# A streaming-encoder trunk in float32 on one core: four kinds of DVE blocks put behind the wide weight splits of their chunk

## The reference

```
h      = rmsnorm(x);  proj = h @ w_in
o_a    = sparse attention with an indexer (8 heads of 128)
o_b    = sliding-window attention (16 heads of 64, sinks)
gates  = sigmoid(h @ w_gate)                  # 2 x 2048 columns: g_a, g_b
merged = g_a * (o_a @ w_branch_a) + g_b * (o_b @ w_branch_b)
x      = x + merged @ w_out
x      = x + square(relu(rmsnorm(x) @ w_up)) @ w_down     # 2048 -> 8192 -> 2048
```

## Time and profile before

| what | us |
|---|---|
| median of three runs | 2659.25 |
| the profiled execution | 2660.85 |
| span of its trace (first to last instruction) | 2659.0 |
| PE busy | 2646.0 |
| PEld busy | 2219.8 |
| DVE busy | 2080.4 |
| ACT busy | 1451.0 |

### The profile page before, as it was taken

One profiled execution on the slowest core, in us unless ns is written; L12 is line 12 of the kernel. 1 busy time (PEld: TensorE's weight loads), 2 busy tenths in 40 slices (PEclk: granted clock), 3 DMA queues, 4 the chain that ended last, 5 costly groups with the idle time before them and its releaser, 6 DMA issues.

```text
span 2659.0 us, 37301 instructions
## 1 busy us (share of the span) xinstructions
PE 2646.0 (100%) x13432; PEld 2219.8 (83%) x13432; DVE 2080.4 (78%) x3099; ACT 1451.0 (55%) x1863; POOL 233.0 (9%) x408
## 2 busy tenths in 40 slices
PE   9999999999999999999999999999999999999998
PEld 7788778888888888888888887788888888888887
DVE  5677678977898997987756766789678989989875
ACT  5545555545565655645455455555456556556554
POOL 0103110000100100100010021100000001000000
PEclk9999999999999999999999999999999999999999
DMA  7887775776775766767677677667677767667574
GB/s 248 240 240 223 224 227 188 226 237 235 237 230 190 246 219 207 241 205 237 227 238 226 223 226 224 215 199 235 221 247 240 224 204 245 211 215 229 195 248 152
DMA packets 185092, 594.52 MB, mean 224 GB/s; under 512 B 25576, under 2 KB 43540, under 8 KB 184784
## 3 DMA queue, kind: packets, MB, share of 16 engines
q1 hardware_dynamic: 161936, 530.65, 61.2%
q0 software_dynamic: 22448, 61.16, 8.4%
q10 hardware_dynamic: 528, 0.37, 0.1%
HBM read 544.58 MB, written 47.48 MB: 223 GB/s over the span
## 4 chain that ended last, share of the span: by engine, by line
PE 96%; DVE 2%; DMA 1%; issue 0%; ACT 0%; SPq 0%; POOLq 0%; POOL 0%; ACTq 0%
PE acc L590 24%; PE acc L592 24%; PE acc L591 24%; PE att L558 2%; PE att L560 2%; PE att L559 2%; PE acc L558 2%; PE acc L560 2%; PE acc L559 2%; PE acc L608 1%; PE acc L607 1%; PE acc L606 1%; PE turn L559 1%; PE turn L560 1%; PE turn L558 1%; DMA raw<-in_w_main 0%
## 5 line engine op out<-in xcount | busy, mean ns | idle before, releaser
L1362 DVE TENSOR_TENSOR w_lo<-raw,w_hi 128x1024 fp32r<-128x1024 f32 (+1 forms) x778 | 933.5, 1211 | 372.0 <-ACT w_hi L934 367.8
L934 ACT ACTIVATE w_hi<-raw 128x1024 fp32r<-128x1024 f32 (+1 forms) x778 | 812.5, 1051 | 622.3 <-PE acc L592 437.8
L590 PE MATMUL acc<-w_hi,h_hl 128*128 128x512 f32 x1848 | 734.7, 398 | 1.1 <-DVE w_lo L1362 1.0
L592 PE MATMUL acc<-w_hi,h_hl 128*128 128x512 f32 x1848 | 729.0, 394 | 0.0
L591 PE MATMUL acc<-w_lo,h_hl 128*128 128x512 f32 x1848 | 728.7, 394 | 0.0
L590 PEld LDWEIGHTS acc<-w_hi,h_hl 128*128 128x128 f32 x1848 | 347.8, 188 | 83.6 <-issue 4.9
L592 PEld LDWEIGHTS acc<-w_hi,h_hl 128*128 128x128 f32 x1848 | 347.8, 188 | 81.6
L591 PEld LDWEIGHTS acc<-w_lo,h_hl 128*128 128x128 f32 x1848 | 348.2, 188 | 76.1
L590 PE MATMUL acc<-w_hi,o_hl 128*128 128x512 f32 x912 | 360.4, 395 | 0.0
L591 PE MATMUL acc<-w_lo,o_hl 128*128 128x512 f32 x912 | 360.0, 395 | 0.0
L592 PE MATMUL acc<-w_hi,o_hl 128*128 128x512 f32 x912 | 359.6, 394 | 0.0
(11 more groups left out here) (298 smaller groups left out, 3629.9 us busy)
## 6 DMA issues: line engine op xcount, KB each, us to landing
raw<-in_w_main SPq DMA_DIRECT2D x928, 512.0 KB, 4.3
scratch<-spread POOLq DMA_DIRECT2D x36, 512.0 KB, 3.3
moved<-scratch POOLq DMA_DIRECT2D x144, 128.0 KB, 5.0
scratch<-spread SPq DMA_DIRECT2D x31, 512.0 KB, 2.9
moved<-scratch SPq DMA_DIRECT2D x124, 128.0 KB, 3.2
scratch_p<-spread POOLq DMA_DIRECT2D x16, 384.0 KB, 4.5
moved<-scratch_p POOLq DMA_DIRECT2D x64, 96.0 KB, 4.3
raw<-in_w_misc SPq DMA_DIRECT2D x16, 336.0 KB, 4.0
```

The lines of the kernel that those rows point to most:

```text
L590: nc.tensor.matmul(o, a_hi, hi[:, kk], start=(k == 0), stop=False)
L592: last = nc.tensor.matmul(o, a_lo, hi[:, kk], start=False, stop=fin)
L934: nc.scalar.activation(w_hi[s][:, 0:2 * width], raw[r][:, 0:2 * width], ACT.Copy).then_inc(hi_ready, 1)
L1362: nc.vector.tensor_tensor(w_lo[s][:, 0:2 * width], raw[r][:, 0:2 * width], w_hi[s][:, 0:2 * width].bitcast(F32), ALU.subtract).then_inc(lo ...
```

## The change

In the gate units of the mixed stage `take_branch_a` and `take_branch_b` run behind the wide subtract of c3 and no longer in front of it. In the branch units `hi_moved` and `lo_moved` run behind the split of the third chunk and no longer behind that of the first. In the feed-forward loop four DVE blocks go from in front of a wide subtract to behind it.

```diff
@@ ACT, mixed stage
                     unit(l * CHUNKS + (C_MIXB + 12 * n + 8), 4, at={3: lambda n=n: gate_side(n)},
-                         then={0: lambda n=n: hi_moved(l, E_M + n - 1, m_dst(n - 1, 0))} if n else ())
+                         then={2: lambda n=n: hi_moved(l, E_M + n - 1, m_dst(n - 1, 0))} if n else ())
@@ DVE, mixed stage
                     unit(l * CHUNKS + (C_MIXB + 12 * n), 8,
-                         take=(lambda n=n: take_branch_b(n - 1)) if n else (lambda: take_branch_a(3)),
+                         then={3: (lambda n=n: take_branch_b(n - 1)) if n else (lambda: take_branch_a(3))},
                          wide=WIDE_GATE, steps=gate_steps(n))
                     then = {3: lambda n=n: add_up_sides(0, 0, n)}
                     if n:
-                        then[0] = lambda n=n: lo_moved(l, E_M + n - 1, m_dst(n - 1, 0), m_dst(n - 1, 1))
+                        then[2] = lambda n=n: lo_moved(l, E_M + n - 1, m_dst(n - 1, 0), m_dst(n - 1, 1))
@@ DVE, feed-forward loop
-                        {2: lambda: u_moved(g, 0), 4: lambda: spread_u(g, 1), 7: lambda: u_sums_lo(g, 0)}, WIDE_UP[2], steps_at(g, AT_UP2))
+                        {3: lambda: u_moved(g, 0), 5: lambda: spread_u(g, 1), 7: lambda: u_sums_lo(g, 0)}, WIDE_UP[2], steps_at(g, AT_UP2))
-                    run(g * 64 + (C_MLP + 40), {3: lambda: add_up_sides(g, 0, NBLK + 1), 7: third_and_spread},
-                        {7: lambda: u_sums_lo(g, 3)}, WIDE[0], steps_at(g, WIDE_AT[0]))
+                    run(g * 64 + (C_MLP + 40), {7: third_and_spread},
+                        {3: lambda: add_up_sides(g, 0, NBLK + 1), 7: lambda: u_sums_lo(g, 3)}, WIDE[0], steps_at(g, WIDE_AT[0]))
-                    run(g * 64 + (C_MLP + 56), {7: lambda: take_down(g, 1, end + 56)}, (), WIDE[2], steps_at(g, WIDE_AT[2]))
+                    run(g * 64 + (C_MLP + 56), (), {7: lambda: take_down(g, 1, end + 56)}, WIDE[2], steps_at(g, WIDE_AT[2]))
```

## The result

| | before | changed |
|---|---|---|
| median, us | 2659.15 (10 runs) | 2667.06 (10 runs) |
| lowest to highest | 2657.93 to 2661.80 | 2665.10 to 2669.51 |
| profiled execution | 2660.85 | 2666.92 |
| its span | 2659.0 | 2665.2 |

The ratio is 1.0028, with a 95% interval of 1.0020 to 1.0037: the changed kernel is slower by 7.9 us in the medians. The forecast was 2659.0 us in a range of 2656.4 to 2661.7, so the measured time lies outside it.

The account below looks back on a forecast made before the run. PE was taken as the bound, fed nearly everywhere. From the profiled execution, 2660.85 - 1.28 + 0.42 = 2660.0 us; from the median, 2659.7 without the stall, 2658.4 with it; middle taken, 2659.0, range 2656.4 to 2661.7.

Parts of the forecast that it names:

- The stall at c6 goes, -1.28 us: Layer 1, second gate unit: c7's load goes out 3.7 us earlier, so PE's late start at c6 goes, -1.28 us.
- The wide subtract waits 0.07 us for ACT: Mixed-stage gate units: c3's wide subtract waits for ACT's w_hi, PE pays at c4; six blocks at 0.07 us, +0.42 us.
- POOL's move comes 2.0 us later, at no cost: Behind the moved block, POOL's store and the four fetches waiting for it come 2.0 us later; no cost in the sum.
- hi_moved and lo_moved at nothing: Two chunks later, each changes places with two splits; PE needs their output only in the output projection; cost nothing.
- The loop at nothing: Four feed-forward loop places: subtracts up to 0.6 us later stay within PE's reserve; cost 0, gain 0.
- the collision only moves on: Rival: later move slows the branch unit's first load, a 1.8 us stall returns; 2661.8 or 2661.0 us; chance 0.11.
- held by ACT: Rival: at c3 the wide subtract waits for a late w_hi, delaying c4 in six blocks; 2665.6 us; chance 0.03.
- The signs of being wrong: PE waiting 0.3 us at c4 in six blocks, branch loads over 9 us, late loop starts, time under 2654 or over 2665.

Follow-up runs that it names:

- the pieces alone: Kernel before with only hi_moved and lo_moved placed two chunks later in the branch units: median 2660.56 us, ratio 1.0009.
- the loop alone: Kernel before with only the change's four edits of the feed-forward loop: median 2658.11 us, ratio 0.9999.
- the three with the sum first: Kernel before with add_up_sides in front of the branch unit's last split: 2656.12 and, repeated, 2657.40 us; with the four loop edits added, 2656.92 us.

## Why the prediction was wrong

- **The stall at c6 goes, -1.28 us: right as a mechanism.** In the changed trace c7's load of the second gate unit of layer 1 goes out at 1776.5, while c4 starts only at 1782.93, and nothing waits for it. As a gain on the median it hardly counts: the sum of the new stalls alone, 8.0 us, is the whole difference of 7.9 us. The stall was one execution's: in the traces of the pieces alone, the loop alone and the three with the sum first, where this load goes out as before and the move is no later, PE loses 0.28 us at that chunk at most.
- **The wide subtract waits 0.07 us for ACT: right.** Its start follows that of c2's `w_lo` by 1.22 us (1774.43 after 1773.21) where the block had followed by 1.14.
- **POOL's move comes 2.0 us later, at no cost: the step that failed.** The prediction followed the moved block to its consumers on PE, and costed the move's other effect, its share of the DMA engines, only as a rival. There it priced the first load of the branch unit, against PE's reserve at that chunk, and got 1.8 us once. The runs show the second load hit: it takes 7.3 to 7.5 us in the four blocks in front of the late c4, where it took 5.1 to 7.2. PE pays 1.75 to 2.22 us behind each of them, 8.0 us in all.
- **The reserve that was compared was the wrong one.** The first load had 8.2 us in the kernel before and PE still found that chunk ready. PE's distance at the delayed chunk is no cover when DVE has next to no gap between that chunk and one with no reserve. c4 without reserve was read correctly, but it was held only against a late ACT at c3, never against a late load of the unit in front.
- **hi_moved and lo_moved at nothing: at most a small error.** In the kernel before, `lo_moved` filled the time in which DVE waits for a load. The run with the pieces alone was 1.5 us slower (interval from 0 to 0.18%), which may be scatter.
- **The loop at nothing: right.**
- **Rival "the collision only moves on": right in mechanism, wrong on the load and in size.** It had the first load of the branch unit pay, where the first is spared and the second pays, and one stall where there are four. Its placed time is also 0.2 us off its own sum (2659.0 + 1.8 = 2660.8, not 2661.0). The Trainium skill's rule behind it ("DMA: Bandwidth & Descriptors", Queues, rings and completion order: DMA engines take turns between queues with work) agrees in kind with these traces: the loads that meet the fetches take longer in either kernel, and with a quarter of the fetched rows they take less.
- **Rival "held by ACT": its ending was near (2665.6), its mechanism not what happened;** the step of the wide subtract is 0.08 us longer, not 0.9.
- **The signs of being wrong did not find this failure.** PE waits at c4 in four places and not in six, and no load of a branch chunk takes over 9 us. A time over 2665 was to mean that the reading of PE's starts was wrong; that reading found every stall.

What stays open: why c7's load once took 6.4 us in the kernel before. No run here was made to settle that.

## What to carry to other kernels

When an edit delays a block, follow its DMAs too: note which loads they will stand beside at the new time, and price the load that is held by the reserve of the next place downstream with none, along the engine that passes it on, not by the reserve of the chunk itself. An engine that has next to no gap between two points, as DVE here with 0.43 us in the 16 us before c4, turns a wait in front of them into lateness behind; work that stands in such a wait is well placed and should not be moved out of it. The cheap way to test a suspected DMA collision is to leave the order alone and move fewer bytes.

## What the runs showed of the hardware that was not expected

1.9 us of offset between a 512 KB move through HBM and the 512 KB loads beside it decide which loads are slow. Over the six blocks of the mixed stage that have a move, us from issue to landing:

| load of the branch unit | before | changed |
|---|---|---|
| first | 5.0 to 8.2 | 3.2 to 4.9 |
| second | 5.1 to 7.2 | 6.5 to 7.5 |
| third | 3.7 to 5.0 | 5.4 to 6.4 |
| fourth | 3.4 to 4.2 | 4.7 to 5.7 |

With a quarter of the fetched rows, in the changed order, the second takes 4.4 to 5.7 us and the third 4.3 to 4.5.
